# Where VectorE does the last two products of retention inside the first steps of attention

## The reference, cut to what matters

```python
for i in range(DEPTH):
    x_rq, x_rk, x_rv, x_rg, x_cq, x_ckv, x_kr, x_gq, x_gk, x_gv = split_proj(hx, w_in[i])
    o_ret = retention_out(bidir_retention(rq_x, rk_x, rv_x, ret_log_decay[i], state_fwd, state_bwd),
                          x_rg, ret_gn_w[i])
    o_mla = attend(mq_x, jnp.concatenate([mk_c, mk_x], axis=2), jnp.concatenate([mv_c, mv_x], axis=2))
    o_gqa = attend(gq_x, jnp.concatenate([gk_c, gk_x], axis=2), jnp.concatenate([gv_c, gv_x], axis=2))
    mix_x = jnp.concatenate([o_ret, merge_heads(o_mla), merge_heads(o_gqa)], axis=-1) @ w_out[i]

def attend(q, k, v):
    def block(qi):                     # 128 queries of one head
        s = jnp.einsum('bkgqd,bksd->bkgqs', qi, k).astype(F32) * scale
        p = jax.nn.softmax(s, axis=-1).astype(v.dtype)
        return jnp.einsum('bkgqs,bkse->bkgqe', p, v)

def retention_out(o, g, gn_w):         # the gate and the norm at the end of retention
    on = merge_heads((of - mu) * lax.rsqrt(var + EPS)) * gn_w.astype(F32)
    return (jax.nn.silu(g.astype(F32)) * on).astype(g.dtype)
```

## Time and profile before

| | |
|---|---|
| median of 3 runs | 3468.09 us (3467.81 to 3469.75) |
| the profiled execution, its own time | 3467.65 us |
| its span in the trace | 3465.8 us |
| mean granted TensorE clock | 0.997 |
| TensorE matmuls | 3398.0 us busy, 98% of the span |
| TensorE weight loads | 2863.9 us, 83% |
| VectorE | 2282.8 us, 66% |
| ScalarE | 1254.1 us, 36% |
| GpSimd | 1010.4 us, 29% |
| attention's entry in layer 0 / layer 1 | 474 to 490 us / 2287 to 2303 us of the span |

### The profile page before, as it was taken

One profiled execution on the slowest core, in us unless ns is written; L12 is line 12 of the kernel. 1 busy time (PEld: TensorE's weight loads), 2 busy tenths in 40 slices (PEclk: granted clock), 3 DMA queues, 4 the chain that ended last, 5 costly groups with the idle time before them and its releaser, 6 DMA issues. The chain is left out here.

```text
span 3465.8 us, 49569 instructions
## 1 busy us (share of the span) xinstructions
PE 3398.0 (98%) x18300; PEld 2863.9 (83%) x18300; DVE 2282.8 (66%) x3527; ACT 1254.1 (36%) x2128; POOL 1010.4 (29%) x1121
## 2 busy tenths in 40 slices
PE   8999999999999999999999999999999999999998
PEld 4888888888888888888888788889998788888886
DVE  6574567886278888888855543478992656656566
ACT  4332356775231111111122432356773322222222
POOL 1232310011423333333334212410014344343433
PEclk9999999999999999999999999999999999999999
DMA  6455463222112222222110424462112111111111
GB/s 242 151 186 195 139 181 79 53 69 69 44 49 73 73 73 73 73 73 73 54 37 31 170 91 155 141 192 63 48 51 87 37 54 43 49 48 42 48 42 61
DMA packets 96241, 304.30 MB, mean 88 GB/s; under 512 B 11872, under 2 KB 38624, under 8 KB 93920
## 3 DMA queue, kind: packets, MB, share of 16 engines
q1 hardware_dynamic: 96096, 302.34, 27.0%
HBM read 239.12 MB, written 63.18 MB: 87 GB/s over the span
## 5 line engine op out<-in xcount | busy, mean ns | idle before, releaser
L131 POOL TENSOR_TENSOR wlo<-raw,whi 128x256 fp32r<-128x256 f32 x516 | 509.0, 1018 | 921.1 <-ACT whi L119 919.1
L2260 DVE SCALAR_TENSOR_TENSOR xT<-down_acc,mod,xT 128x512 f32<-128x512 f32 (+1 forms) x800 | 515.9, 695 | 221.9 <-PE down_acc L192 219.5
L1981 POOL TENSOR_TENSOR hid_lo<-y,hid_hi 128x256 fp32r<-128x256 f32 (+1 forms) x189 | 159.9, 878 | 642.7 <-ACT hid_hi L2157 642.7
L2146 ACT ACTIVATE up<-up_acc 128x512 f32<-128x512 f32 (+1 forms) x210 | 116.0, 554 | 614.0 <-PE up_acc L192 613.7
L190 PE MATMUL up_acc<-mix_hi,whi 128*128 128x512 f32 (+1 forms) x875 | 327.8, 375 | 1.4 <-ACT up L2146 0.7
L192 PE MATMUL up_acc<-mix_hi,wlo 128*128 128x512 f32 (+1 forms) x875 | 326.2, 373 | 0.0
L191 PE MATMUL up_acc<-mix_lo,whi 128*128 128x512 f32 (+1 forms) x875 | 325.1, 372 | 0.0
L191 PE MATMUL up_acc<-late_lo,whi 128*128 128x512 f32 (+1 forms) x860 | 317.6, 369 | 0.0
L192 PE MATMUL up_acc<-late_hi,wlo 128*128 128x512 f32 (+1 forms) x860 | 317.2, 369 | 0.0
L190 PE MATMUL up_acc<-late_hi,whi 128*128 128x512 f32 (+1 forms) x860 | 317.1, 369 | 0.0
L192 PE MATMUL down_acc<-hid_hi,first_wlo 128*128 128x512 f32 (+1 forms) x825 | 314.4, 381 | 0.0
(11 more groups left out here) (334 smaller groups left out, 7610.5 us busy)
## 6 DMA issues: line engine op xcount, KB each, us to landing
raw<-in_w_rest SPq DMA_DIRECT2D x112, 512.0 KB, 3.7
norm_buf<-in_w_ada SPq DMA_DIRECT2D x52, 768.0 KB, 4.4
first_raw<-in_w_rest SPq DMA_DIRECT2D x57, 512.0 KB, 3.8
proj_scratch<-stage SPq DMA_DIRECT2D x18, 640.0 KB, 5.0
raw<-in_w_first SPq DMA_DIRECT2D x21, 512.0 KB, 6.2
ada_raw<-in_w_ada SPq DMA_DIRECT2D x6, 1536.0 KB, 13.8
xT<-proj_scratch SPq DMA_DIRECT2D x4, 1920.0 KB, 9.3
xT<-in_xT SPq DMA_DIRECT2D x8, 640.0 KB, 24.8
```

Of the source, the lines that this page charges most:

```text
L131: m = nc.gpsimd.tensor_tensor(self.lo[k][:, x:x + 256], self.raw[k][:, x:x + 256], self.hi[k][:, x:x + 256].bitcast(f32), ALU.subtract)
L1981: m = nc.gpsimd.tensor_tensor(hid_lo[:, x:z], y[1][:, x:z], hid_hi[:, x:z].bitcast(f32), ALU.subtract)
L2146: nc.scalar.activation(up[half][:, pc:pc + w], ub[c][:, :w], ACT.Copy).then_inc(up_evac, 1)
L2260: nc.vector.scalar_tensor_tensor(xs, db[g % DB][:, :w], mod_of(layer, 5, m, c), xs, ALU.mult, ALU.add).then_inc(added, 1)
```

## The change

VectorE's two products of retention's last turn (lines 1657 and 1662) move from behind first_part(2) of loop turn 0 to behind first_part(3) of loop turn 1, in both layers. Nothing else changes.

```diff
@@ -1376,7 +1376,7 @@
                         low(n)
                     if n + 2 < N:
                         first_part(n + 2)
-                    if n == 0:
+                    if n == 1:
                         ret.finish(dve, ret.turns - 1)
                     if n % 2 == 0 and 0 <= n // 2 - 2 < NG:
                         normalise(n // 2 - 2)
```

## The result

| | before | changed |
|---|---|---|
| median of 22 runs each | 3469.65 us (3465.98 to 3472.25) | 3474.41 us (3469.74 to 3476.31) |
| profiled execution | 3467.65 us, span 3465.8 | 3475.79 us, span 3474.0 |
| mean granted clock | 0.997 | 0.994 |

The ratio of the changed kernel to the one before is 1.0015, with a 95% interval of 1.0009 to 1.0020: slower by 0.15%, or by 4.8 us between the medians, and clear of noise. The direction is as forecast and the change stays within 0.2%; its size is twice the forecast 2.25 us, and 3474.41 lies 0.6 us above the range.

What follows compares the result with a forecast made beforehand. TensorE, busy 98% of the span, was taken to bound the kernel. Later low(2) and scores(4) in the two layers, 1.29 + 0.96 = 2.25 us, gave 3470.3 us; the range took in 3467.6 to 3473.8 us.

Steps and rivals of the forecast that it cites:

- The wait that ends last: Ahead of low(2): VectorE waits for the moved store's landing, so low(2) starts 1.29 us later in layer 0, 0.96 in layer 1.
- The gain ahead of low(1): Without the pair ahead of it, low(1) and then scores(3) start 0.54 us earlier in layer 0, 0.86 in layer 1.
- Layer 1: Attention's entry in layer 1: low(2) and scores(4) come 0.96 us later, waiting for the store's landing of 2.2 us.
- Layer 0: Attention's entry in layer 0: low(2) and scores(4) come 1.29 us later, waiting for the store's landing of 2.2 us.
- The clock rival: Granted clock falls behind TensorE's new 1.66 us gap ahead of scores(4); in both layers 3.4 us more, 3473.7 us; chance 0.05.
- The sum: Delays of scores(4) in both layers, 1.29 + 0.96 = 2.25 us slower; 1.4 to 2.9 us with the ends.
- head 1 never waited for its loads: Head 1's loads in layer 1, issued 4.1 us later, still land 2.7 us early; rival of late loads 3475.7 us, chance 0.03.
- ScalarE's and TensorE's waits for the product: ScalarE's high part of step 2 and TensorE's first values wait for the moved pair; neither was to cost anything.
- TensorE made up for nothing behind scores(4): Steps behind scores(4) keep their distances, so its delay of 1.29 and 0.96 us stays in the total.

Runs made afterwards that it cites:

- with the packet out of the way: Changed kernel plus 128 already-met waits on TensorE and 64 on ScalarE in layer 0's retention, which moved the instruction packets' times: 3483.36 us, a single run.
- the run where they can be counted: Changed kernel, but SyncE waits for the last store's landing before issuing the 1920 KB load behind it: 3472.42 us against 3469.03, ratio 1.0009.

## Why the prediction was right or wrong

- **The mechanism was right.** "The wait that ends last" is the store's landing: without it the loss is gone (ratio 0.9994, its interval below that of the changed kernel).
- **The gain ahead of low(1)** was forecast as 0.54 and 0.86 us and is 0.69 and 0.99 (from low(0) to low(1) 4.60 to 3.91 and 4.92 to 3.93), since low(1) came 1.13 us behind maximum(2), not 1.26. It did not survive maximum(3), as forecast.
- **Layer 1**: 0.96 us later forecast, 0.8 measured, with a gap of 1.53 us for 1.66 and a landing of 2.1. This part of the sum holds.
- **Layer 0 is the term that failed.** I put 1.29 us, from a landing of 2.2 us, since 18 of 18 stores had taken 2.0 to 2.2. It took 4.3, and scores(4) came 3.2 us later. The rest of the term holds: with the packet out of the way and a landing of 2.1, scores(4) came 1.1 us later. Those 18 were issued at other moments: none had an instruction packet go out between its issue and its landing, and the two at the entry went out at 488.5 and 490.7 in the trace of before, well behind the store at 483.63. I moved the store by 4 us and kept its price, without asking what the DMA engines do at the new time. The list of DMA queues names the instruction queues, and a narrow window would have shown both packets.
- **The clock rival** had a chance of 0.05 and happened. Its premise, a gap of 1.66 us, held in layer 1 only; the gap of 3.66 us followed from the first error. Its price, 1.7 us a layer, was 1.7 in layer 1 and 2.9 in layer 0, where TensorE was at the lower level for longer than in the earlier trace rows.
- **The sum.** The waits make 3.2 + 0.8 = 4.0 us. The lowest of 22 runs moved by 3.8 us (3465.98 to 3469.74) and the median by 4.8; I read the rest as the lower clock, which the order of before pays too: it fell behind 3 of the 6 gaps ahead of scores(3) in entries with that order, though behind neither in the trace that I predicted from. That reading is argued, not shown.
- **The base.** The forecast of 3470.3 stands on a median of three runs, 3468.09; over 22 runs the same kernel has 3469.65. So 1.6 of the 4.1 us between forecast and result belong to the base and 2.5 to the change. I also took 0.2% as what can be told from no change; with 22 runs each, 0.15% was.
- **What held:** head 1 never waited for its loads; ScalarE's and TensorE's waits for the product cost nothing (the first values start 0.6 us sooner behind low(0) than before); TensorE made up for nothing behind scores(4).

## What to carry to other kernels

A wait that is free because its transfer landed long ago is priced at nothing only where it stands; move the transfer's issue towards the wait and its whole latency appears, and with it whatever the DMA engines do at the new time. When a step is moved, follow what it releases on every queue to the last reader of the memory that it holds, and give the tile another place if that reader is the one that waits. On TensorE a gap costs its length and possibly the clock behind it.

## What the runs showed of the hardware that I had not expected

- A 192 KB store that lands in 2.0 to 2.2 us took 3.3 to 4.3 when a 16 KB instruction packet went out 1.0 to 2.0 us behind its issue: in the run where they can be counted, a sixteenth of the store's packets went out only behind it. Moving either of the two brought 2.1 and 2.2 back.
- The granted clock behind gaps of 1.4 to 2.0 us at attention's entry fell in 5 of 12 cases over the profiled executions (the order of before included) and kept 1.00 in 7, with gaps as alike as 1.53 (fell), 1.53 and 1.55 (did not). Behind the six gaps of 2.9 us or more it fell each time.
